# Hybrid attention step on one core: output loads respaced, a seventh weight slot, eight weight sums moved to accumulating loads

## Reference

```python
h = rms_norm(x, norm_pre)
p = h @ w_in                      # 12 column groups: q, k, v, gate of three head groups
oa = stick_breaking(qa, ka, va)   # 12 heads, causal over everything
ob = band_attention(qb, kb, vb, ..., alibi, sinks)   # own and 2 previous chunks
oc = band_attention(qc, kc, vc, ..., rel_bias)       # own and 8 previous chunks
mixed = concat(oa*silu(ga), ob*silu(gb), oc*silu(gc))
y = x + rms_norm(mixed @ w_out, norm_post)           # mixed: tokens x 2048, w_out: 2048 x 2048
```

## Time and profile before

| | |
|---|---|
| median of 3 runs | 1928.67 us (1927.08 to 1930.82) |
| the profiled execution, its own time | 1934.61 us |
| its span, first to last instruction | 1932.9 us |
| mean granted TensorE clock | 0.993 |
| PE busy | 1891.8 us, 98% of the span |
| DVE, ACT, POOL busy | 1246.4, 673.4, 56.7 us |
| DMA traffic | 318.35 MB, mean 165 GB/s |

### The profile page before, as it was taken

The page is one execution under the profiler, slowest core; times in us unless marked ns, Lnnn a source line. Parts: engine busy times, 40 slices in busy tenths (PEclk is TensorE's granted clock), DMA queues, the critical chain, the costliest instruction groups (busy, mean ns, idle before and its releaser), DMA issues.

```text
span 1932.9 us, 31215 instructions
## 1 busy us (share of the span) xinstructions
PE 1891.8 (98%) x12592; PEld 1735.3 (90%) x12592; DVE 1246.4 (64%) x2235; ACT 673.4 (35%) x1235; POOL 56.7 (3%) x119
## 2 busy tenths in 40 slices
PE   6999999999999999999999999999999999999998
PEld 5999999999999999999999999999999987776776
DVE  7368787887878778454454444465445576765878
ACT  7233334343334334122222122233223353334463
POOL 4000000000000000000000000000000000000150
PEclk9999999999999999999999999999999999999999
DMA  6456777776776777666657666465446568766696
GB/s 245 117 121 137 161 159 163 147 152 150 150 163 149 164 149 162 140 140 153 134 126 158 138 141 136 113 147 126 101 100 135 135 246 313 242 228 240 222 256 229
DMA packets 887368, 318.35 MB, mean 165 GB/s; under 512 B 623417, under 2 KB 850505, under 8 KB 883881
## 3 DMA queue, kind: packets, MB, share of 16 engines
q1 hardware_dynamic: 884152, 307.64, 64.5%
q0 software_dynamic: 3072, 8.73, 2.2%
HBM read 227.23 MB, written 96.20 MB: 167 GB/s over the span
## 4 chain that ended last, share of the span: by engine, by line
PE 85%; DVE 9%; DMA 3%; ACT 2%; issue 1%; SPq 0%; POOL 0%; DVEq 0%
PE ps L1277 21%; PE ps L1278 20%; PE ps L1279 20%; PE ps L1471 4%; PE ps L1472 4%; PE ps L1473 4%; PE ps L1369 3%; PE ps L1449 3%; PE ps L1419 2%; PE ps L1341 2%; DVE arena L1956 1%; DMA r_extra<-in_w_out_dram 1%; DMA b_out<-in_w_out_dram 1%; DVE act_lo L1823 1%; DVE arena L1816 1%
## 5 line engine op out<-in xcount | busy, mean ns | idle before, releaser
L1277 PE MATMUL ps<-act_hi,w_hi 128*128 128x352 f32 x2688 | 877.8, 327 | 0.8 <-DVE arena L1856 0.8
L1279 PE MATMUL ps<-act_hi,w_lo 128*128 128x352 f32 x2688 | 863.1, 321 | 0.0
L1278 PE MATMUL ps<-act_lo,w_hi 128*128 128x352 f32 x2688 | 862.8, 321 | 0.0
L1277 PEld LDWEIGHTS ps<-act_hi,w_hi 128*128 128x128 f32 x2688 | 504.4, 188 | 21.0 <-issue 15.7
L1278 PEld LDWEIGHTS ps<-act_lo,w_hi 128*128 128x128 f32 x2688 | 505.4, 188 | 0.0
L1279 PEld LDWEIGHTS ps<-act_hi,w_lo 128*128 128x128 f32 x2688 | 504.4, 188 | 0.0
L1583 ACT ACTIVATE w_hi<-w_raw 128x512 fp32r<-128x512 f32 x224 | 139.4, 624 | 371.7 <-DMA w_raw<-in_w_in_dram 371.5
L1831 DVE TENSOR_TENSOR w_lo<-w_raw,w_hi 128x512 fp32r<-128x512 f32 x224 | 150.4, 672 | 52.8 <-ACT w_hi L1583 52.5
L1650 ACT ACTIVATE arena<-arena,small 128x257 f32<-128x257 f32 (+6 forms) x180 | 101.3, 565 | 198.2 <-DVE small L1994 198.2
L2154 DVE STREAM_TRANSPOSE arena<-arena 128x1024 f32<-128x1024 f32 (+4 forms) x100 | 132.5, 1325 | 38.3 <-ACT arena L1772 37.5
L1772 ACT ACTIVATE arena<-arena 128x1024 f32<-128x1024 f32 (+1 forms) x60 | 61.1, 1019 | 236.4 <-DVE arena L1968 236.4
(11 more groups left out here) (173 smaller groups left out, 2073.2 us busy)
## 6 DMA issues: line engine op xcount, KB each, us to landing
w_raw<-in_w_in_dram SPq DMA_DIRECT2D x176, 256.0 KB, 3.4
weight_scratch<-arena SPq DMA_DIRECT2D x216, 128.0 KB, 3.4
arena<-weight_scratch SPq DMA_DIRECT2D x54, 512.0 KB, 4.6
b_out<-in_w_out_dram SPq DMA_DIRECT2D x72, 256.0 KB, 4.3
w_raw<-in_w_out_dram SPq DMA_DIRECT2D x70, 256.0 KB, 3.0
w_s<-in_w_out_dram SPq DMA_DIRECT2D x16, 1024.0 KB, 7.4
w_raw<-in_w_in_dram SPq DMA_DIRECT2D x96, 128.0 KB, 3.1
weight_scratch<-arena SPq DMA_DIRECT2D x80, 132.0 KB, 4.0
```

Source lines behind the costliest of these rows:

```text
L1277: mm(bank(g, GN), wh, ah, start=(k == 0), stop=False)
L1278: mm(bank(g, GN), wh, al, start=False, stop=False)
L1279: last = mm(bank(g, GN), wl, ah, start=False, stop=(k == KT - 1))
```

## The change

- `R_RING` goes from 6 to 7: a third `r_extra` slot, and each piece is loaded one piece earlier against its use.
- The five later loads of mixed activations move from pieces 1 to 5.9 of the plan to pieces 8.2 to 17.2. The decode products use their rows in the natural order, stand 4 pieces apart (after r = 15, 19, ... 75) instead of 5 (10, 15, ... 85), and the decode rows are ended first (`FINISH`).
- `fill_y` leaves SP's queue. POOL issues eight copies of 64 rows and the decode rows' copy during the attention units of group C.
- `BY_DMA` covers r = 96 to 111: the eight sums of stage 12 are made by accumulating loads of POOL's queue too.
- The residual loads 0 to 3 move from pieces 99.5 to 102.5 to pieces 86.2 to 90.7.
- PE does row group j = 3 of a stage's first piece after the first three of the second piece.
- The gains of the second norm are loaded at piece 30.2 instead of 9.1.

```diff
-    return at_piece(max(r - 5, 2.6 + 0.3 * (r - 6)))
+    return at_piece(max(r + 1 - R_RING, 2.6 + 0.3 * (r - 6)))
...
-    return (TICKS - 8.9, TICKS - 8.8, TICKS - 5.9, TICKS - 5.8, at_piece(1), at_piece(1.2), at_piece(1.4), at_piece(1.6), at_piece(5.9))[n]
+    return (TICKS - 8.9, TICKS - 8.8, TICKS - 5.9, TICKS - 5.8, at_piece(8.2), at_piece(10.2), at_piece(12.2), at_piece(14.2), at_piece(17.2))[n]
...
-        elif engine == "pool" and r >= TAIL0:
-            plan.append((summed_at(r), "add_out", 0, r))
+        elif engine == "pool" and BY_DMA[r]:
+            plan.append((summed_at(r) - (0 if r >= TAIL0 else 0.6), "add_out", 0, r))
...
-            if SUMMED[r] and r < TAIL0:
+            if SUMMED[r] and not BY_DMA[r]:
                 plan.append((summed_at(r), "sum_out", 0, r))
...
-        plan += [(at_piece(104.3 + 0.1 * n if n > 3 else 99.5 + n), "residual", 0, n) for n in range(len(PLAIN))]
-        plan += [(at_piece(50 + 2.5 * n), "fill_y", 0, n) for n in range(3)]
-        plan += [(at_piece(3.9), "store_mixed", NU - 1, 0), (at_piece(9.1), "post_gains", 0, 0)]
+        plan += [(at_piece(104.3 + 0.1 * n if n > 3 else 86.2 + 1.5 * n), "residual", 0, n) for n in range(len(PLAIN))]
+        plan += [(at_piece(4.2), "store_mixed", NU - 1, 0), (at_piece(30.2), "post_gains", 0, 0)]
...
-R_RING, B_RING = 6, 5
+R_RING, B_RING = 7, 5
 LEAD = 3
-FINISH = (4, 5, 6, 7, TT, 0, 1, 2, 3)
+FILLS = 2 * NC
+FINISH = (TT, 4, 5, 6, 7, 0, 1, 2, 3)
...
-SAMPLE_ORDER = tuple(range(KH, KT)) + tuple(range(KH))
-SAMPLE_AFTER = [10 + 5 * v for v in range(KT)]
+SAMPLE_ORDER = tuple(range(KT))
+SAMPLE_AFTER = [15 + 4 * v for v in range(KT)]
...
+BY_DMA = [r >= TAIL0 - KH for r in range(PIECES)]
...
             for r in range(LEAD, TAIL0):
                 operands_out(r)
-                for j in range(4):
+                for j in range(3):
                     out_mm(r, j)
+                if r % KH == 1:
+                    out_mm(r - 1, 3)
+                if r % KH:
+                    out_mm(r, 3)
...
+            for n in range(FILLS):
+                pool.wait_ge(pv_done, step_no(NA + n // 2, 1 + 3 * (n % 2)))
+                a, b = (4 * P + n * (4 * P // FILLS), 4 * P + (n + 1) * (4 * P // FILLS))
+                gp.dma_start(y_prompt[0, a:b, :], x_prompt[0, a:b, :]).then_inc(y_filled, 16)
+            gp.dma_start(y_sample[0], x_sample[0]).then_inc(y_filled, 16)
```

More of the change, by code:

```diff
@@ L346, in output_tasks @@
             plan.append((piece_out_at(r), "piece_out", 0, r))
-        elif engine == "pool" and r >= TAIL0:
-            plan.append((summed_at(r), "add_out", 0, r))
+        elif engine == "pool" and BY_DMA[r]:
+            plan.append((summed_at(r) - (0 if r >= TAIL0 else 0.6), "add_out", 0, r))
         elif engine == "act":
-            plan.append((summed_at(r) + (4.4 if r >= TAIL0 else 0.7), "hi_out", 0, r))
+            plan.append((summed_at(r) + (4.4 if r >= TAIL0 else 2.9 if BY_DMA[r] else 0.7), "hi_out", 0, r))
         elif engine == "dve":
-            if SUMMED[r] and r < TAIL0:
+            if SUMMED[r] and not BY_DMA[r]:
                 plan.append((summed_at(r), "sum_out", 0, r))
-            plan.append((summed_at(r) + (5.0 if r >= TAIL0 else 0.3 if r == 3 else 0.6 if 6 <= r < 9 else 1.3), "lo_out", 0, r))
+            plan.append((summed_at(r) + (5.0 if r >= TAIL0 else 3.5 if BY_DMA[r] else 0.3 if r == 3 else 0.6 if 6 <= r < 9 else 1.3), "lo_out", 0, r))
     for i in range(7):
@@ L365, in output_tasks @@
         if engine == "sp":
-            plan.append((sample_at(n - 1) if n else at_piece(6), "rows_out", 0, n))
+            plan.append((sample_at(n - 1) if n else at_piece(9.5), "rows_out", 0, n))
     for n in range(NCH):
@@ L551 @@
 SUMMED = [len(RIGHT[STAGE[r // KH][0]]) > 1 for r in range(PIECES)]
-SUMS_BY = list(itertools.accumulate(SUMMED))
+BY_DMA = [r >= TAIL0 - KH for r in range(PIECES)]
+SUMS_BY = list(itertools.accumulate(a and not b for a, b in zip(SUMMED, BY_DMA)))
 LEFT_SUMS_BY = list(itertools.accumulate(len(LEFT[m]) > 1 for m in ORDER for _ in range(KH)))
-RAW_OUT = [16 * sum(1 + SUMMED[x] for x in range(r % R_RING, r + 1, R_RING)) if r < TAIL0 else 16 for r in range(PIECES)]
+RAW_OUT = [16 * sum(1 + (SUMMED[x] and not BY_DMA[x]) for x in range(r % R_RING, r + 1, R_RING)) if r < TAIL0 else 16 for r in range(PIECES)]
 def final_adds(t, n):
@@ L655, in build @@
         w_s = place("w_s", [P, D], F32, 0, 12736)
-        r_extra = [place(f"r_extra{i}", [P, PIECE], F32, 0, 14784 + PIECE * i) for i in (0, 1)]
-        r_extra_lo = [place(f"r_extra_lo{i}", [P, PIECE], F32R, 0, 14784 + PIECE * i) for i in (0, 1)]
-        r_extra_hi = [place(f"r_extra_hi{i}", [P, PIECE], F32R, 0, 15808 + PIECE * i) for i in (0, 1)]
+        EXTRA_AT = ((14784, 15808), (15296, 16320), (11008, 11520))
+        r_extra = [place(f"r_extra{i}", [P, PIECE], F32, 0, c) for i, (c, _) in enumerate(EXTRA_AT)]
+        r_extra_lo = [place(f"r_extra_lo{i}", [P, PIECE], F32R, 0, c) for i, (c, _) in enumerate(EXTRA_AT)]
+        r_extra_hi = [place(f"r_extra_hi{i}", [P, PIECE], F32R, 0, c) for i, (_, c) in enumerate(EXTRA_AT)]
         ended = [place(f"ended{i}", [P, PIECE], F32, 0, 14784 + PIECE * i) for i in range(4)]
@@ L825, in build @@
         tail_added = [sem(f"tail_added{i}") for i in range(KH)]
+        sum_added = [sem(f"sum_added{i}") for i in range(KH)]
         tail_high, tail_low = sem("tail_high"), sem("tail_low")
@@ L1181, in residual @@
                 sp.dma_start(residual_of(n), x_prompt[0, P * t:P * t + P, c].rearrange("p (k c) -> p k c", c=PIECE)).then_inc(res_in[n], 16)
[L1183 to L1189, removed]
             def store_y(t, half):
@@ L1244, in _ @@
                     residual(n)
-                elif what == "fill_y":
-                    fill_y(n)
                 elif what == "store_y":
@@ L1251, in _ @@
             sp.wait_ge(v_stored, 32 * (NA + NB + NC))
-            sp.wait_ge(y_filled, 16 * 3)
+            sp.wait_ge(y_filled, 16 * (FILLS + 1))
             sp.wait_ge(y_stored, 16 * len(PLAIN))
@@ L1657, in high_out @@
                     return
-                if SUMMED[r]:
+                if BY_DMA[r]:
+                    act.wait_ge(sum_added[r % KH], 16)
+                elif SUMMED[r]:
                     act.wait_ge(r_summed, SUMS_BY[r])
@@ L2244, in add_out @@
                 col = 1024 * cols + PIECE * c
-                gp.dma_start(r_raw(r), w_out_v[:, K_ROWS[KH * inner + k], col:col + PIECE], accum_op=ALU.add).then_inc(tail_added[k], 16)
+                gp.dma_start(r_raw(r), w_out_v[:, K_ROWS[KH * inner + k], col:col + PIECE], accum_op=ALU.add).then_inc(tail_added[k] if r >= TAIL0 else sum_added[k], 16)
             def variance(tt):
@@ L2274, in add_y @@
             def add_y(t, half):
-                pool.wait_ge(y_filled, 16 * 3)
+                pool.wait_ge(y_filled, 16 * (FILLS + 1))
                 pool.wait_ge(scaled, ADDED.index((t, half)) + 1)
```

## The result

| | before | after |
|---|---|---|
| median (range) of six runs each | 1927.3 us (1926.22 to 1930.82) | 1934.44 us (1933.65 to 1935.14) |
| the profiled execution, its own time | 1934.61 us | 1933.65 us |
| first `add_y` | 1837.19 | 1832.67 |
| first matmul of r = 104 | 1902.25 | 1901.25 |
| from r = 104 to the end of the span | 30.65 us | 30.65 us |

The changed kernel takes 1.0033 times as long [1.0022, 1.0044]: slower by 0.33%, where 1920 us and "faster" were predicted. The two profiled executions, 1 us apart the other way, mislead: that of before is slower than any timed run of this kernel.

The account below looks back on a forecast made before the run. PE, busy 98% of the span, was taken as the bound, with DMA bounding the stretch before r = 104. -6.3 - 6.3 + 2.8 + 1.2 = -8.6 from the median 1928.67 gave 1920 us, own range 1915 to 1925.

Parts of the forecast that it names:

- the rule alone: Stage 12's accumulations cost 0.72 us per tile as before; stretch 2.6 us shorter, sum about 1915.
- the priced sum: Stage 12's tiles cost 1.40 us of DMA accumulated, 0.72 loaded; stretch to r = 104 2.8 us longer, total 1920.
- the second rival: Stage 12: accumulations queue behind `add_y`, loads behind residual loads; first sum 6 to 7 us late; 1928 us, chance 0.17.
- the two gains: Ending PE's waits at r = 6 and at stage 8, with the low clock after them: 6.3 us each.
- The median of the runs is 5.9 lower than this execution: Shift from the profiled 1934.61 us to the median 1928.67, from which 8.6 was subtracted.
- four residual loads, 5.8. Sum 62.4: DMA work from the first `add_y` before the change, ending at 1899.6; residual loads count 5.8 after it too.
- so DMA is the real bound of this stretch: First `add_y` to r = 104, before: the DMA sum closes to 1 us with the last accumulation's landing at 1900.7.
- Decode products. ... Nothing: Decode products four pieces apart instead of five: same 16, same cost, nothing, with 0.8 us left at worst.
- order of ending: off the path, 0: Ending the decode rows first lies off the path and costs 0 us.
- The third rival: Low clock through stage 12 from waits at nearly every piece: 19 us more for 32 groups; 1939 us, chance 0.10.
- a clock below 0.8: Sign through stage 12 that the prediction of 1920 us is wrong.
- no wait above 1 us up to r = 90: Sign of being right: PE has no wait above 1 us from r = 3 to 90.

Follow-up runs that it names:

- e1: The kernel before, unchanged, profiled a second time: 1931.52 us in this execution.
- e13: e7 with DVE's two additions that free the bank of r = 96's last row group eight operations earlier: 1922.04 us, 0.997.
- e4: The kernel before with only the y fills moved to POOL's queue: 1924.91 us, 0.9973.
- e7: e6 with the sums of stage 12 made by DVE again instead of accumulating loads: 1921.85 us, 0.9964.
- e6: e5 with residual loads 0 to 3 back at plan pieces 99.5 to 102.5: 1925.91 us, 0.9983.
- e5: The changed kernel with decode products five pieces apart, the old order of ending and the first `rows_out` at piece 6: 1930.98 us, 1.0013.
- e9: e7 with PE's row groups in their natural order again: 1920.5 us, 0.9963.
- e8: The kernel before with stage 12's sums by accumulating loads and, with them, later high and low parts, ring of six: 1934.09 us, 1.0027.
- e3: The changed kernel with residual loads 0 to 3 back at plan pieces 99.5 to 102.5: 1930.37 us, 1.0005.
- e12: e7 with four of stage 12's eight sums, r = 100 to 103, made by accumulating loads: 1925.03 us, 0.9982.

## Why the prediction was wrong

The kernels form a chain from before to after, in which each step is one part of the change. Beside it the prediction's terms (us, differences of medians). The chips of e1 to e13 differ by up to 0.4 in the median of before; the first result has 1927.3 there. With each kernel against its own before, the last step is +4.8 and the sum +7.1:

| step | kernels | predicted | measured |
|---|---|---|---|
| fills to POOL | before 1928.4, e4 1924.9 | -6.3 | -3.5 |
| mixed loads, seventh slot, row group 3, gains, order of the decode rows' loads | e4, e7 1921.85 | -6.3 | -3.1 |
| stage 12's sums by accumulation | e7, e6 1925.9 | +2.8 | +4.1 |
| residual loads early | e6, e5 1931.0 | 0 | +5.1 |
| decode rows: spacing, order of ending | e5, after 1934.4 | +1.2 | +3.5 |
| sum | | -8.6 | +6.1 |

**Right.** The waits at r = 6 and stage 8 end, no wait came near the mixed loads, and the fills cost nothing that shows among the attention units (the first output matmul starts at 1578.06, before at 1578.70). PE waits in stage 12 on DMA, whose share stays at 1.06 to 1.09, and no longer on DVE's additions. By the rule alone that the prediction cites from the Trainium skill (page "DMA: Bandwidth & Descriptors", section "Issuing engines are not separate DMA queues") the sum would have been about 1915. The share over 1 with both queues agrees with it, but it gives no price for an accumulation: the priced sum was nearer, and wrong as well. The delay of the first sum is that of the second rival, "6 to 7 us late": it was 6.4. Of its two reasons one held, "the loads of r = 94 to 97 behind 2.1 MB of residual loads"; the queue behind `add_y` did not, for POOL stood idle 17.4 us before that accumulation. It had 0.17.

**Wrong: the two gains.** The step that failed is "-6.3 - 6.3" together with "The median of the runs is 5.9 lower than this execution". The gains were read in an execution of 1934.61 us, which is above every timed run of before (the highest of 80 is 1933.83). What made it slow lay ahead of the first `add_y`, where both waits are; a second profile has 2.2 instead of 3.5 at r = 6. In e1 the two waits with the low clock behind them cost 3.9 and 6.2 us, by what PE's starts are more than 0.227 us apart from 1595.45 to 1602.14 and from 1749.79 to 1759.22; that execution is 3.1 above its median, which leaves 7.0. Taken together the two steps gave 6.6. So the mechanism was right and the size wrong: by these two executions, part of the 12.6 was already in the 5.9, and was subtracted twice. Within the two executions the gain is there, as the start of stage 10 shows. Why before scatters over 8 us, and the changed kernel over 1.5 in six runs, isn't shown: timed runs have no trace.

**Wrong: "four residual loads, 5.8. Sum 62.4", and "so DMA is the real bound of this stretch".** The sum puts the residual loads into both kernels, so that moving them costs nothing. That it closed to 1 us was no proof that they bound the end. Loads that nothing waits for may land behind the start of r = 104, as in e6, and the cost of moving them shows in e6 and e5, 66.0 against 71.9 us of stretch. Early, they stand ahead of r = 96 in SP's queue: 4.9 of the 6.4 us. And e7, with the sums and residual loads of before, takes 62.4 us where before takes 65.1, whose one long wait there is behind an addition by DVE: DMA as the bound of before's stretch isn't shown.

**Wrong: "Decode products. ... Nothing" and "order of ending: off the path, 0".** The decode rows' statistics and scaling now come first on ACT, DVE and POOL, ahead of four row blocks. ACT then makes the high part of the left operand for r = 87 behind scales of the row blocks, 6.0 us later than in e5 (first the changed kernel, then e5):

```profile
1837.56 0.61 ACT L1666 ACTIVATE l_hi<-l_sum 128x512 fp32r<-128x512 f32 x1
```

```profile
1831.59 0.61 ACT L1666 ACTIVATE l_hi<-l_sum 128x512 fp32r<-128x512 f32 x1
```

PE waits 2.6 us, 4.4 with the low clock behind it, and the first `add_y` is 7.0 us later than in e5. Two decode products now lie ahead of stage 10, 2.4 us; the sum has one, 1.2. By the medians 3.5 us stay. Spacing and order were not separated; a kernel with only one of them wasn't tried, so it is argued from the order that the early ending makes ACT late.

**The size of the accumulations.** The stretch was forecast at 67.9 us and measured at 68.6. That is luck: it starts with the late `add_y`, at a later point of PE's work, and holds 218 matmuls by the trace, 252 in e5. There it is 71.9, 4.0 above the sum. The residual loads are not the difference, for the sum has them: without their 5.8 it is 62.1, and e6 measures 66.0. The accumulations alone were +2.8 in the sum and +4.1 measured. The sum has no term for the low clock that follows the waits it creates: from the first `add_y` to r = 104, PE waits 5.7 us in e6 and 4.2 in e7, 1.5 more, and what its starts are more than 0.227 us apart grows by 3.4. The third rival had this mechanism, at 19 us for a whole stage. It came for 9.8 us of matmuls and cost 4.6. The prediction's sign of it, a clock below 0.8, was there from 1860 to 1890 us, and its sign of being right, no wait above 1 us up to r = 90, failed at r = 87.

The miss of 14.4 us is then the sum's 14.7: 6.0 in the gains, 1.3 in the accumulations, 5.1 in the residual loads, 2.3 in the decode rows. The 0.3 between them come from the medians of before that the two start from.

## What to carry to other kernels

Where the DMA share is at 1, moving a load that nobody waits for ahead of loads that somebody waits for cost 5.1 us here: count what stands in the queue ahead of the first late tile, not only the sum. Before an engine is relieved, ask whether what takes the work over has time left; here an accumulated tile cost two plain ones (1.40 against 0.72 us of all 16 engines), and even half of them lost. Price a gain against the median of several runs before it is subtracted from one: an execution slower than all the timed ones can hold waits that the median does not have in full. And compare two kernels from the same point of PE's work, not from an event that the change itself moves.

The version to keep is e9: the change's ring, mixed loads, gains and fills, without its accumulations, early residual loads, decode order and row group order. It takes 0.9963 of before's time, and 14 us less than the changed kernel. e7 can't be told from it.

## What the runs showed of the hardware

In the fourteen traces, from the start of the output stage on, each of PE's 22 waits of 2.5 us or more was followed by matmuls 0.43 us apart. Of three waits between 2.1 and 2.4 us one was, the 2.15 us before 1597.99 in e1, from 1599.16 on; those of e5 and e8 were not. Of the shorter ones none was that stood by itself. In the changed kernel it is so at once after the 6.4 us, and from 0.9 us after the 2.6 us of stage 10 on, for 3.4 us (starts 1839.81 to 1843.18); in e3 it begins 1.2 us after the wait of 2.50. In e13, whose seven waits are of at most 1.8 us and add up to 6.1, the granted clock of 1860 to 1890 us is 1.00 throughout. In e7, with 4.9 us of waits and one of 3.2 among them, it is 0.94. What e13 saves in clock it loses in waits: the two take the same time. That the clock alone, with equal waits, would pay was not tested.

Accumulating loads of 256 KB took a median of 8.0 us to land in the changed kernel from 1855 to 1900 us, 10.0 at most (below), against 6.7 in the kernel before. The plain load of r = 96 took 13.8 up to POOL's next issue; the median of such loads in the earlier trace rows is 10.0.

```profile
DMA to landing us min/median/max: 3.7/8.0/10.0
```

Four single runs took 2071.66 to 9422.91 us, all in kernels with accumulating loads in stage 12 (e5, e8, e12 twice). The kernel before also has accumulations, in its last stage, and had none such in 80 runs. In all, the kernels with accumulating loads in stage 12 had 4 in 61 runs, those without none in 127. The cause is open.
